# The z projection of a latent-attention layer with tokens on partitions, and the attention scores of the last layer as fp32r passes with two of four weight scalings moved to ScalarE

## The reference, cut to what matters

```python
# first layer: z is 2048 of the 3136 columns of one input projection
proj = x @ w_in                       # [tokens, 1088 for c_q, c_kv and the rotary key | 2048 for z]
...
y = (attention_out * silu(z)) @ w_out

# last layer, mixer a: 8 heads of width 64, 2 kv heads
s_s = einsum('btgrd,bgtkld->bgrtkl', qblk, ksel) * scale + bias     # selected blocks
s_w = einsum('btgrd,bsgd->bgrts', qblk, kw) * scale + bias          # window
p   = masked_softmax(s); o = einsum(p, v)
o   = g[..., 0:1] * o_cmp + g[..., 1:2] * o_slc + g[..., 2:3] * o_win
```

## Time and profile before

| | |
|---|---|
| median of three runs | 1941.08 us (1940.8 to 1941.73) |
| the profiled execution | 1940.91 us, span 1939.4 us |
| TensorE busy | 1933.9 us, 100% of the span |
| VectorE, ScalarE busy | 1358.0 us (70%), 1001.2 us (52%) |
| DMA | 353.21 MB, 182 GB/s mean |
| granted TensorE clock | 1.00 throughout |

### The profile page before, as it was taken

The page is one execution under the profiler, slowest core; times in us unless marked ns, Lnnn a source line. Parts: engine busy times, 40 slices in busy tenths (PEclk is TensorE's granted clock), DMA queues, the critical chain, the costliest instruction groups (busy, mean ns, idle before and its releaser), DMA issues.

```text
span 1939.4 us, 25500 instructions
## 1 busy us (share of the span) xinstructions
PE 1933.9 (100%) x10006; PEld 1647.0 (85%) x10006; DVE 1358.0 (70%) x2011; ACT 1001.2 (52%) x1433; POOL 0.2 (0%) x4
## 2 busy tenths in 40 slices
PE   9999999999999999999999999999999999999999
PEld 7889988988888888898888888888888888888887
DVE  6756778887555687998788887489666444666654
ACT  5645554675556554585566655444444334444442
POOL 0000000000000000000000000000000000000000
DMA  8454325455544455545534345555555555555563
GB/s 327 178 193 175 129 90 193 176 196 185 192 172 152 174 195 196 195 174 198 217 114 157 116 155 196 197 190 185 187 193 205 198 202 192 190 185 195 186 227 108
DMA packets 51706, 353.21 MB, mean 182 GB/s; under 512 B 5652, under 2 KB 7196, under 8 KB 9860
## 3 DMA queue, kind: packets, MB, share of 16 engines
q1 hardware_dynamic: 50016, 348.84, 49.0%
q10 hardware_dynamic: 1572, 2.75, 0.4%
HBM read 349.47 MB, written 2.11 MB: 181 GB/s over the span
## 4 chain that ended last, share of the span: by engine, by line
PE 94%; DVE 4%; ACT 1%; issue 0%; ACTq 0%; DVEq 0%
PE bank L1208 94%; DVE WL L2137 2%; DVE AR L2314 0%; ACT WH L1635 0%; DVE AR L2427 0%; DVE XP L2310 0%; DVE AR L2424 0%; DVE XP L2412 0%; PE bank L1353 0%; DVE AR L2303 0%; DVE AR L2338 0%; DVE AR L2337 0%; ACT XP L1766 0%; ACT L1648 0%; PE bank L1587 0%
## 5 line engine op out<-in xcount | busy, mean ns | idle before, releaser
L1635 ACT ACTIVATE WH<-raw 128x1024 fp32r<-128x1024 f32 x649 | 683.5, 1057 | 655.8 <-PE bank L1208 648.1
L2137 DVE TENSOR_TENSOR WL<-raw,WH 128x1024 fp32r<-128x1024 f32 x649 | 784.8, 1222 | 316.3 <-ACT WH L1635 312.7
L1208 PE MATMUL bank<-XP,WH 128*128 128x512 f32 (+2 forms) x1584 | 498.5, 389 | 0.4 <-DVE XP L2412 0.2
L1208 PE MATMUL bank<-WH,FP 128*128 128x512 f32 x1408 | 434.8, 389 | 0.0
L1208 PEld LDWEIGHTS bank<-XP,WL 128*128 128x128 f32 x1504 | 281.8, 187 | 59.4 <-issue 0.7
L1208 PEld LDWEIGHTS bank<-WH,FP 128*128 128x128 f32 x1408 | 264.3, 188 | 55.7 <-DVE WL L2137 1.0
L1208 PE MATMUL bank<-XP,WL 128*128 128x256 f32 (+1 forms) x1504 | 308.5, 279 | 0.1
L1208 PE MATMUL bank<-WH,XP 128*128 128x512 f32 (+1 forms) x960 | 299.5, 388 | 0.3 <-DVE WL L2137 0.3
L1208 PE MATMUL bank<-WL,FP 128*128 128x512 f32 x704 | 273.9, 389 | 0.0
L1208 PEld LDWEIGHTS bank<-XP,WH 128*128 128x128 f32 (+1 forms) x1584 | 248.0, 187 | 7.4 <-issue 1.4
L1208 PE MATMUL bank<-WH,AP 128*128 128x512 f32 x704 | 217.0, 389 | 0.0
(11 more groups left out here) (339 smaller groups left out, 1632.0 us busy)
## 6 DMA issues: line engine op xcount, KB each, us to landing
raw<-in_W SPq DMA_DIRECT2D x326, 1024.0 KB, 4.8
out<-XT ACTq DMA_DIRECT2D x8, 256.0 KB, 2.1
raw<-in_W SPq DMA_DIRECT2D x3, 512.0 KB, 6.8
X<-in_x SPq DMA_DIRECT2D x3, 512.0 KB, 12.4
AR<-rv SPq DMA_DIRECT2D x1, 1024.0 KB, 5.8
cst<-in_cst SPq DMA_DIRECT2D x1, 899.5 KB, 11.2
raw<-in_W SPq DMA_DIRECT2D x2, 256.0 KB, 4.3
AR<-in_sgu SPq DMA_DIRECT2D x1, 512.0 KB, 5.7
```

Source lines behind the costliest of these rows:

```text
L1208: return pe.matmul(o, lhsT, rhs, start=start, stop=stop)
L1635: ac.activation(w_slot(WH, s), raw_half(hf), ACT.Copy).then_inc(s_hi, 1)
L2137: tt(w_slot(WL, s), raw_half(pl.half_of[s]), w_slot(WH, s).bitcast(F32), ALU.subtract).then_inc(s_lo, 1)
```

## The change

**z.** The weights are cut into 4 blocks of 512 features, and a tile now keeps the tokens stationary (2 token halves) and moves 512 weight columns: six matmuls of 512 columns for 128x512 weights. ScalarE applies silu while it reads PSUM (two halves for each block, tokens on partitions, into a buffer ZR), and VectorE turns the result back with 4x4 transposes of 32-row blocks (`z block`, 16 of them with four instructions each). The last four z blocks are turned in section mla, one in each of the first four attention steps there; the copies and adds of z and the separate silu passes go.

**Scores of the last layer.** A key tile is split once into high (KH) and low (KL) parts (`k high` on ACT, `k low` on DVE, `k turn` on ACT). For each head, `q high` (ACT, 64x256) and `q low` (DVE, 64x256) write one tile QS whose one half of rows is the high part of q and whose other half is the low part. a0 becomes four fp32r matmuls, two of 512 columns and two of 256, and waits for `q low` of its head.

**Weight scalings.** In a3 VectorE does reciprocal, gates and the two 128x128 scalings; ScalarE does the two 128x256 ones, waiting for the VectorE product. a4 waits for both.

```diff
-    t_blocks("mla_w_in", [r(1088 + 128 * b, 128) for b in range(16)], DM)
+    t_blocks("mla_w_in", [r(1088 + 512 * n, 512) for n in range(4)], DM)
...
-for _s in [Stage("c", ...), Stage("z", 16, 16, "dve"),
+for _s in [Stage("c", ...), Stage("z", 4, 16, "act", 0, 512),
...
     def a0(h):
         say("a0", h)
+        if h < 7:
+            say("q high", h + 1)
+            say("q low", h + 1)
+        if h == 1:
+            say("k turn")
...
@@ pe_program, a0
-                    q = blk(QZ, h % 4)
-                    k = kswn[h // 4]
-                    mm(X1[:, 0:512], q[:, 128:256], k, True, True)
-                    mm(Y1[:, 0:256].rearrange(...), q[:, 0:128], k.rearrange(...)[:, :, 0:128], True, True).then_inc(s_n1, 1)
+                    pe.wait_ge(s_kl, 3 + h + 1)
+                    q = QS[h % 2]
+                    mm(two(X1[:, 0:512]), q[:, 128:256], k, True, False)
+                    mm(two(X1[:, 0:512]), q[:, 128:256], kl, False, True)
+                    mm(two(Y1[:, 0:256]), q[:, 0:128], k[:, :, 0:128], True, False)
+                    mm(two(Y1[:, 0:256]), q[:, 0:128], kl[:, :, 0:128], False, True).then_inc(s_n1, 1)
@@ pe_program, a4
                     pe.wait_ge(s_n4, h + 1)
+                    pe.wait_ge(s_n4a, h + 1)
@@ act_program
+            def z_silu(n):
+                b, half = divmod(n, 2)
+                ac.wait_ge(*done("z", b))
...
+                ac.activation(ZR[b % 2][:, 512 * half:512 * half + 512], bank[pl.bank_of["z", b, half]][:, :],
+                              ACT.Silu).then_inc(s_out["act"], 1)
...
+            def q_high(h):
+                sl = slice(64 * (h // 4), 64 * (h // 4) + 64)
+                if h >= 2:
+                    ac.wait_ge(s_n1, h - 1)
+                ac.activation(QS[h % 2][sl, :], blk(QZ, h % 4)[sl, :], ACT.Copy).then_inc(s_qh, 1)
...
+                elif what == "a3":
+                    i = h % 4
+                    ac.wait_ge(s_nw, h + 1)
+                    for s in (0, 1):
+                        ap = seg(h)[s]
+                        ins = ac.activation(ap, ap, ACT.Copy, scale=sm[i][:, s:s + 1])
+                    ins.then_inc(s_n4a, 1)
@@ dve_program
+            def z_block(n):
+                b, a = divmod(n, 4)
+                if a == 0:
+                    dv.wait_ge(*outed("z", b, 1))
+                src = ZR[b % 2].rearrange("p (f t) -> p f t", f=8)
+                dst = Z[:, 1024 * b:1024 * b + 1024].rearrange("p (f t) -> p f t", f=8)
+                for c in range(4):
+                    ins = dv.transpose(dst[32 * c:32 * c + 32, :, 32 * a:32 * a + 32],
+                                       src[32 * a:32 * a + 32, :, 32 * c:32 * c + 32])
+                ins.then_inc(s_zt, 1)
...
+            def q_low(h):
+                dv.wait_ge(s_qh, h + 1)
+                tt(QS[h % 2][to, :], blk(QZ, h % 4)[sl, :], QS[h % 2][sl, :].bitcast(F32), ALU.subtract).then_inc(s_kl, 1)
...
@@ a3
                     chain(dv.reciprocal(sm[i], sm[i]))
-                    chain(tt(sm[i], sm[i], GX[:, 6 * h:6 * h + 4], ALU.mult))
-                    for s, ap in enumerate(seg(h)):
+                    tt(sm[i], sm[i], GX[:, 6 * h:6 * h + 4], ALU.mult).then_inc(s_nw, 1)
+                    dv.wait_ge(s_nw, h + 1)
+                    for s in (2, 3):
+                        ap = seg(h)[s]
                         ins = ts(ap, ap, sm[i][:, s:s + 1], None, ALU.mult)
                     ins.then_inc(s_n4, 1)
```

More of the change, by code:

```diff
@@ L441, in plan, with z_after, told, z_by_token @@
     go(cp)
-    p.big, p.turn = [0, 1, 2], 1
+    p.big, p.turn = [1, 2, 3, 7], 0
     p.section("z")
-    zp = p.proj(st["z"])
+    def z_after(b):
+        return {1: [("z", b, 0)], 3: [("z", b, 1)], 5: [("z block", 4 * b)], 7: [("z block", 4 * b + 1)],
+                9: [("z block", 4 * b + 2)], 11: [("z block", 4 * b + 3)]}
+    def told(steps, at):
+        for what in steps.get(at, ()):
+            if what[0] == "z":
+                p.out(st["z"], what[1], what[2])
+            else:
+                say(*what)
+    def z_by_token():
+        for y, _ in enumerate(p.proj_tm(st["z"], 1, out=False)):
+            b, at = divmod(y, 16)
+            if b:
+                told(z_after(b - 1), at)
+            yield
+    zp = z_by_token()
     say("c squares")
@@ L455, in plan @@
     go(zp, 4)
+    say("silu table")
     say("krope cos")
@@ L460, in plan @@
     say("krope fill")
[L461 to L466, removed]
     go(zp)
+    p.big, p.turn = [0, 1, 2], 0
     p.section("mla")
@@ L505, in plan @@
     for step in range(16 + len(stages) - 1):
+        if step < 4:
+            say("z block", 12 + step)
         for s in range(len(stages) - 1, -1, -1):
@@ L658, in plan @@
              23: [("qk rstd", 1)], 25: [("qk scaled", 1), ("qk squares", 2)], 27: [("zeros", 2), ("qk rstd", 2)],
-             29: [("qk scaled", 2)]}
+             29: [("qk scaled", 2)], 30: ["k high"]}
     for at in range(31):
@@ L672, in plan @@
     for step in (("nsa gates", 0), ("cmp gelu", 0), ("zeros", 3), ("zeros", 0)):
+        if step[0] == "cmp gelu":
+            say("k low")
         say(*step)
@@ L703, in d5 @@
         say("d5", h)
+        if h == 6:
+            say("q high", 0)
         if h == 7:
             say("sg gelu", 0)
+            say("q low", 0)
     p.pipe(8, ["d0", "d1", "d2", "d3", "d4", d5, "d6"], gating_and_cz(), 38, (0, 3, 5))
@@ L1695, in act_program @@
                     high_scaled(4 * n, (CP, KP)[n], (cq, ckv)[n])
[L1696 to L1703, removed]
+                elif what == "silu table":
+                    ac.preload_act_table(ACT.Silu)
+                elif what == "z out":
+                    z_silu(n)
             for what, n in pl.steps["mla"]:
@@ L1965, in act_program @@
                     rstd(rs6, bank[7][:, :], 64, 0).then_inc(s_qrs, 1)
+                elif what == "k high":
+                    ac.wait_ge(s_qsc, 3)
+                    for g, half in ((1, 1), (0, 0), (0, 1)):
+                        ac.activation(KH[g][64 * half:64 * half + 64, :], KN[64 * g:64 * g + 64, :],
+                                      ACT.Copy).then_inc(s_kh, 1)
                 elif what == "cmp gelu":
@@ L2022, in act_program @@
                     ac.activation(lA[h % 4], zA[h % 4], ACT.Exp).then_inc(s_g5e, 1)
+                elif what == "q high":
+                    q_high(n)
                 elif what == "sg gelu":
@@ L2033, in act_program @@
                     b_half(n)
+                elif what == "q high":
+                    q_high(n)
+                elif what == "k turn":
+                    ac.wait_ge(s_g7, 8)
+                    two = lambda ap: ap.rearrange("p (s k) -> p s k", s=2)
+                    for half in range(2):
+                        ac.activation(KL1[64 * half:64 * half + 64], two(KH[1][0:64, :].bitcast(F32)),
+                                      ACT.Copy).then_inc(s_kh, 1)
+                    ac.wait_ge(s_kh, 5)
+                    ac.activation(KH[1][0:64, :], KH[1][64:128, :].bitcast(F32), ACT.Copy).then_inc(s_kh, 1)
                 elif what == "sg gelu":
@@ L2207, in dve_program @@
                     lo(n)
-                elif what == "z out":
-                    whole("z", n, blk(Z, n))
+                elif what == "z block":
+                    z_block(n)
                 elif what == "c fold":
@@ L2755, in dve_program @@
                        czs.rearrange("p (s n) -> p s n", n=1).broadcast_to([128, 16, 15]), ALU.mult).then_inc(s_cz, 1)
+                elif what == "q low":
+                    q_low(n)
                 elif what == "d2":
```

98 lines of the change are left out of this document (57 added, 41 removed).

## The result

The changed kernel takes **1960.87 us** (median of four runs, 1959.35 to 1961.03), the kernel before, run beside it, 1941.32 us (1940.8 to 1941.73). The ratio is 1.0099, 95% interval 1.0087 to 1.0111: slower by 1.0%. The forecast of 1954.6 us had the direction and the place right and was 6.3 us too low; the time lies 0.9 us above the range of 1940 to 1960.

The account below looks back on a forecast made before the run. TensorE was taken to bound the kernel: 1940.91 - 2.1 (z) - 4.7 (scores) + 20.5 (new waits) = 1954.6 us, 0.7% slower. The forecast's own range was 1950 to 1959, the 8-in-10 range 1940 to 1960.

Parts of the forecast that it names:

- What bounds it: Whole kernel: TensorE, busy 1933.9 of 1939.4 us, so its saved work shortens and its added waits lengthen the kernel.
- z, -2.1 us: z stage: 384 matmuls of 512 columns take 87.1 us instead of 89.2, saving the fixed part of 128 matmuls.
- The cover: z stage: VectorE's added transposes and ScalarE's work stay hidden behind TensorE, so added wait is taken as 0.
- Scores, -4.7 us: Last layer's attention: a0 falls from 1.29 to 0.70 us a head, over eight heads.
- the preparation: Making k high, k low and k turn, early and once: taken as 0, 2.1 us if nothing covered it.
- The new waits, +20.5 us: Last attention: in-order queues with new ScalarE, VectorE and TensorE waits make TensorE wait 21.1 us, against 0.6 before.
- The clock: TensorE's clock, 1.00 in all these stretches, was expected to stay there and left out of the sum.
- the walk: Last attention: the three engines' queues stepped through in order with trace durations, giving 21.1 us of TensorE waits.
- clean gain: Rival: waits stay hidden and only TensorE's own work shrinks, 1934.1 us; chance 0.13.
- only q low hurts: Rival: ScalarE's scalings delay nothing VectorE needs; 6.9 us of waits, 1940.4 us, no change; chance 0.09.
- Worse through z blocks: Rival: delayed b copies and z blocks in the first attention add 1.74 us in four steps, 1961.6 us; chance 0.06.
- f32 price for strided passes: Rival: fp32r passes with strided moving operand run at f32 price, a0 1.4 us, total 1960; chance 0.02.

Follow-up runs that it names:

- five kernels of the account: Changed kernel, 1960.87 us; with scalings behind a2, 1951.44; all on VectorE, 1941.95; ahead of a5 with q low moved, 1939.38; kernel before plus scalings alone, 1954.2.
- the kernel with work in its waits: Changed kernel plus 36 small zero-operand f32 matmuls on TensorE directly ahead of its nine longest waits; 1957.23 us, ratio 1.0083.

## Why the prediction was off

- **What bounds it:** right in the main. TensorE's work, slowed work and waits explain the span to 0.7 us in all five kernels of the account (1.2 with the wait of before taken off). "Nothing later gives it back" held for the kernel before, not for the changed one: its wait at a4(1) took up the 1.3 us of slowed work behind a0(4).
- **z, -2.1 us:** right, 2.0 measured. The cover held: no new wait, VectorE at 71.92 of 87 us.
- **Scores, -4.7 us:** right as TensorE's own time (0.70 us each): from the 512 column matmul before a0 to the 256 column one behind it there are 1047.92 - 1046.75 = 1.17 us in the kernel with all scalings on VectorE, 1.76 before. Of the preparation nothing showed, as assumed.
- **The new waits, +20.5 us:** right in place and order, low in size. Walked 21.1, in the trace 22.3 with the hidden part, and more with the clock kept up: the kernel with work in its waits took 1957.23 us, 2.6 above the 1954.6. (The twelve terms add up to 21.2, and 42.7 us over five steps are 8.5 each; in the trace a0(2) to a0(7) took 46.5 us, 1047.41 to 1093.92, 9.3 each.) "Waits of TensorE for q low" was the wrong name: a0 waits for a1 of the head before, which `q low` holds up in VectorE's queue. The scalings take 0.81 us (1064.14 to 1064.95), not 0.60; my range ended at 0.7, because I halved the duration of a 512 column pass. VectorE's reciprocals (L2969) in the trace stand at 1055.59, 1063.74, 1071.18, 1081.24 and 1094.79, so the rounds are 8.2, 7.4, 10.1 and 13.6 us, where I had 7.6, 7.1, 9.7 and 11.3. The fourth holds the slowest matmuls, those of 1086 to 1090.
- **The clock: the step that failed.** "TensorE's clock is 1.00 in all these stretches and no edit lets it idle for long, so it is left out" stood in the first part, while the walk, in the part on the new waits, had a6(1) idle for 4.7 us and a6(2) for 3.0. The rows of before could not show the fall, because TensorE never idled there; the sentence should have been asked again after the walk. The term was 4.7 us of slowed work by the account, of which the run with work in the waits got back 3.6; the rest was slowed work that the wait of a4(1) took up. With it the sum would have been 1954.6 + 3.6 = 1958.2 us; the other 2.6 of the 6.3 us are the waits above. Either miss alone would have stayed within the range; only both together left it.
- **The rivals:** "clean gain" and "only q low hurts" didn't come; but the second, walked as the change without ScalarE's part, was built, and took 1941.95 us for its 1940.4. "Worse through z blocks" had by chance nearly the right time, 1961.6, for the wrong reason. f32 price for strided passes: not seen.
- **The range:** its upper end was taken from the sizes in the walk and from the rivals, and no case held the clock. With the 3.6 us of the clock on top, the forecast's own range, 1950 to 1959, would have ended near 1963.

## What to carry to other kernels

When work is moved to an engine that runs ahead of the one it comes from, look not at how busy it is but at what stands behind the moved step in its queue: here 0.81 us a head on an engine half idle cost 13 us by themselves, and with the same instructions a few places later (and two `q low` moved) the whole change was 21.5 us faster. An engine that waits in such a queue holds up what stands behind it, even where nobody waits for the moved step itself. A walk of the queues with durations from the trace finds such waits, and their sum to some 15% in the five kernels of the account (with `q low` on GpSimd it had 2.5 us for 4.1), single ones less well (2.3 walked for the 1.29 of a4(1)). When it has found them, ask what the clock does behind each of the long ones, and whether a later wait takes it up.

## What the runs showed of the hardware

- A wait of TensorE of 2.2 to 4.8 us in a stage otherwise dense can be followed by 2.8 to 5.6 us of work at 1.2 GHz, and need not be: it was behind 2.21, 2.56, 2.71, 2.85, 3.06 and 4.83 us, and was not behind 2.06, 2.30 and 3.22 us. What decides is not settled by these runs; the length of the wait alone it is not. A forecast has to count such a wait as a chance: the work lost was 1.3 to 1.7 us behind each of three waits in the changed kernel and 2.8 us behind the one of 3.06 us, and a later wait can take part of it up.
- Small matmuls by a zero operand (64 rows, 256 columns, 0.437 us each) in nine waits went with a clock of 1.00 throughout; with only three waits filled it fell once, behind an idle one of 2.56 us.
- Two 128x256 scalings with a scale from SBUF take ScalarE 0.81 us to the next instruction (1064.14 to 1064.95 in the changed kernel), 0.41 each.
